# The last pair's chunks copied on chip, its stores issued last, and one head sum behind the first output tile

## The chip, the cores and the metric

One core of one Trainium2 chip runs the whole program. The metric is the device time of one execution in microseconds, as the median over runs; runs of the kernel before were 1549.65, 1552.05 and 1554.65 us.

## The reference

The program computes one decoder layer on 1040 tokens (16 meta tokens and 1024 inputs) of width 1024. What matters here, cut down:

```python
xn = rmsnorm(h, g_pre_mix)
p = xn @ w_in                                # RWKV columns | stick-breaking columns
y_a = rwkv7_group(p_rwkv, ...)               # 8 heads x 64: state scan, group norm, bonus, gate
y_b = stick_breaking_group(q, k, v, gain)    # 8 heads x 64: stick-breaking attention, RMSNorm per head
h = h + rmsnorm(concat(y_a, y_b) @ w_out, g_post_mix)
m = square(relu(rmsnorm(h, g_pre_ffn) @ w_ffn_up)) @ w_ffn_down
h = h + rmsnorm(m, g_post_ffn)               # returned without the meta tokens
```

`rwkv7_group` multiplies its normed result by a gate and adds a bonus, both of which are known before the scan. The stick-breaking output `o` is divided by the root of its mean square per head.

## The kernel before

The program has three large stages, each a block: all five engines leave a block together, after the last of them is done.

**`stage_in_proj`** computes the projection in 26 tiles and, beside it, prepares the RWKV heads in four pairs of heads (`PAIRS`; 128 partitions hold two heads of 64). For each pair it makes `fields`, 17 chunks of 64 tokens with five fields each (B, A, R, K, V), and two full rows, `bv` (the bonus) and `gate`. All of these go to DRAM (`chunk_dram`, `bonus_dram`, `gate_dram`). Projected tiles go to `p_dram`, stored by ACT's queue. The last step of `prepare` for a pair, on SP's queue (L352 to L362), waits for all of the pair's work; for the last pair it then calls `start.load_chunk` (L876), which loads chunk 0 of the next stage: of the first three pairs from `chunk_dram`, of the last pair straight from `fields` in SBUF. Then follow the last pair's three stores. Bonus and gate count on `last_small_left`, for which SP waits at the end of its program (L384); the chunk store counts on `left`, which the next stage waits for. POOL ends its program with `start.load_heads` (L888): nine loads of the values, queries and keys of the first attention pair from `p_dram`.

**`stage_mix`** runs the RWKV scan and the attention side by side. The scan takes 17 laps, one chunk each. A lap has a front (products of the chunk's fields `fld[s]` and their exchanged copy `swp[s]`, s = lap mod 2) and a rear (which updates the state and gives `y`). The attention is cut into numbered ticks ("sticks"), and `program` weaves quarters of them between the slots of a lap in one fixed order on every engine. Lap 0 uses the loaded chunk 0. Lap 1 uses `fld1` and `swp1`, which SP loads after it has waited for `left_done` (L1052 to L1054); the same semaphore is waited for by ACT before its first `high_q` (L1181). The first DVE instruction of tick 4 is the clamp at L1318. The first write of ACT into `y_sb` is at L1165 (`m == 0`).

**`stage_tail`** norms and gates `y` and `o`, projects them with `w_out`, adds the residual, and does the FFN. `head_sums` (L2566) are products with a block of ones: `mean(i)` and `var(i)` for `y`, `osum(i)` for `o`, by section i of the tokens. `project_first` (L2604) makes the first token tile from unrounded operands: eight steps of two 128x512 products (L2614), four on `o` and then four on `y`. Between these two halves stand `mean(2)` and `osum(2)`. `osum(2)` waits for ACT's square of `o` (L2008); ACT's logarithm (L2012) waits for `osum(2)`. DVE's `low_of_w` (L2291) of a late weight tile waits until `project_first` has used the tile. DVE's order there is: the last L2291, `scale_o(2)` (L2272, which waits for `ors_done` from ACT), `deviation(2)` (L2250); then ACT squares the deviation (L2018), and `var(2)` on PE waits for that. `project` of tile 1 (L2600) follows `var(2)`.

Of the kernel before, what the change touches and what calls it, by code (L numbers as in the profile page):

```python
# [11 lines left out]
P = 128  # L12
# [3 lines left out]
SEQ = 1024  # L16
# [4 lines left out]
CH = 64  # L21
# [172 lines left out]
def stage_in_proj(nc, start, stored, left, x_dram, meta, gain_row, ident, w_in, raw, masks, p_dram, xh, xl, vecs, mu_low, w_low_up, chunk_dram, gate_dram,  # L194
# [7 lines left out]
    with ExitStack() as ctx:  # L202
# [62 lines left out]
        rkv_loaded, vec_loaded, wlow_loaded, last_small_left = m.sem("rkv_loaded"), m.sem("vec_loaded"), m.sem("wlow_loaded"), m.sem("last_small_left")  # L265
# [41 lines left out]
        def _(sp):  # L307
# [29 lines left out]
            def prepare(h, u):  # L337
# [18 lines left out]
                if i == PAIRS - 1:  # L356
                    start.load_chunk(sp, fields)
                small_left = last_small_left if i == PAIRS - 1 else left
                sp.dma_start(bonus_dram[i], bv[:, 0:SEQ]).then_inc(small_left, 16)
                sp.dma_start(gate_dram[i], gate).then_inc(small_left, 16)  # L360
                sp.dma_start(chunk_dram[i].rearrange("c p f -> p c f"),
                             fields[:, :, :, :].rearrange("p c f n -> p c (f n)")).then_inc(left, 16)  # L362
# [21 lines left out]
            sp.wait_ge(last_small_left, 2 * 16)  # L384
# [6 lines left out]
        def _(pool):  # L391
# [41 lines left out]
            M.wait(pool, PAIRS - 1, "b1")  # L433
            start.load_heads(pool)
# [402 lines left out]
class MixStart:  # L837
# [38 lines left out]
    def load_chunk(self, sp, fields):  # L876
# [3 lines left out]
        chunk = self.chunk_dram[there, 0].rearrange("q p f -> p q f")  # L880
        sp.dma_start(self.fld0[:, there, X_B:X_I, :].rearrange("p q f n -> p q (f n)"), chunk[:, :, 0:3 * CH]).then_inc(self.loaded, 16)
        sp.dma_start(self.fld0[:, last, X_B:X_I, :], fields[:, 0, F_B:F_K, :]).then_inc(self.loaded, 16)
        for h in range(2):
            here, other = slice(h * HD, (h + 1) * HD), slice((1 - h) * HD, (2 - h) * HD)
            sp.dma_start(self.swp0[other, there, :, :].rearrange("p q f n -> p q (f n)"), chunk[here, :, CH:]).then_inc(self.loaded, 16)
            sp.dma_start(self.swp0[other, last, :, :], fields[here, 0, F_A:, :]).then_inc(self.loaded, 16)
# [21 lines left out]
def stage_mix(nc, start, stored, left_done, chunk_dram, p_dram, masks, ident, pc, y_sb, o_sb, w_out, w_raw, w_late, gate_dram, bonus_dram):  # L908
# [29 lines left out]
    with ExitStack() as ctx:  # L938
# [21 lines left out]
        v = [m.sb(f"v{s}", [P, BLOCKS, P]) for s in range(2)]  # L960
        tri = m.sb("tri", [P, P])
# [7 lines left out]
        a = [m.sb(f"a{i}", [P, SBW]) for i in range(4)]  # L969
# [81 lines left out]

# [1806 lines left out]
```

## Time and profile before

| | |
|---|---|
| median of three runs | 1552.05 us (1549.65 to 1554.65) |
| the profiled execution's own time | 1554.16 us |
| its span in the profile | 1552.4 us |
| granted TensorE clock, mean over the span | 0.984 |
| PE / DVE / ACT / POOL busy | 95% / 68% / 52% / 19% |
| DMA | 258.06 MB, mean 166 GB/s |

A row of the profile gives an engine (PE is TensorE, DVE VectorE, ACT ScalarE, POOL GpSimd, SP SyncE; a q behind the name is its queue) and a line of the kernel. Times are from the start of the span. The projection stage ends on PE near 348 us, the mixing stage runs from 360 to 779 us, and the tail follows.

### The profile page before, as it was taken

What the parts mean: (1) busy time and instruction counts of PE and PEld (TensorE: products, weight loads), DVE (VectorE), ACT (ScalarE), POOL (GpSimd) and SP (SyncE); (2) the same over time, 40 slices, a digit from 0 to 9 for tenths busy, and PEclk for the clock granted to TensorE, in tenths of its full rate; (3) what the DMA queues carried; (4) which work ended last, traced back from release to release, by engine and by line L of the source; (5) the groups of instructions that cost most, each with busy time, mean ns of one, the idle gap of its engine ahead of it and who ended that gap; (6) DMA issues with size and microseconds to landing.
All of it is one profiled execution on the core that took longest, in us unless ns stands there. A gap on an engine that the chain in (4) does not pass through costs nothing. (4 is left out here: it accounts for less than half of the span.)

```text
span 1552.4 us, 36775 instructions
## 1 busy us (share of the span) xinstructions
PE 1468.7 (95%) x15392; PEld 1243.9 (80%) x15392; DVE 1049.3 (68%) x1522; ACT 805.4 (52%) x1396; POOL 300.2 (19%) x307
## 2 busy tenths in 40 slices
PE   6999999995998999999889996999999999999998
PEld 6999999995777777777658875878888888888886
DVE  6244436445878887789766769998888665544555
ACT  6254445344777877778665543333333343433452
POOL 6233425340001011010100004543333000100000
PEclk9999999997999999999999998999999999999999
DMA  4433562646613224121244567798777585675553
GB/s 183 143 125 126 184 233 75 233 124 196 145 34 85 54 51 106 40 51 42 80 96 122 144 222 239 271 306 280 265 250 247 193 305 190 231 271 192 194 183 136
DMA packets 120220, 258.06 MB, mean 166 GB/s; under 512 B 9200, under 2 KB 50288, under 8 KB 119808
## 3 DMA queue, kind: packets, MB, share of 16 engines
q1 hardware_dynamic: 115536, 239.33, 47.4%
q10 hardware_dynamic: 3744, 13.85, 2.2%
q0 software_dynamic: 784, 2.65, 0.7%
q8 instruction: 116, 1.90, 0.5%
q14 instruction: 40, 0.33, 0.1%
HBM read 167.67 MB, written 86.85 MB: 164 GB/s over the span
## 5 line engine op out<-in xcount | busy, mean ns | idle before, releaser
L2415 DVE TENSOR_TENSOR tail_tl<-tail_down_raw,tail_th 128x1024 fp32r<-128x1024 f32 x84 | 102.0, 1256 | 96.2 <-ACT tail_th L2097 96.2
L2097 ACT ACTIVATE tail_th<-tail_down_raw 128x1024 fp32r<-128x1024 f32 x84 | 84.4, 1052 | 129.1 <-PE tail_bank L2701 114.5
L2701 PE MATMUL tail_bank<-tail_th 128*128 128x512 f32 x336 | 131.0, 390 | 0.0
L2701 PE MATMUL tail_bank<-tail_th,tail_tl 128*128 128x512 f32 x336 | 131.0, 390 | 0.0
L2701 PE MATMUL tail_bank<-tail_tl,tail_th 128*128 128x512 f32 x336 | 130.7, 389 | 0.0
L689 PE MATMUL inproj_acc<-xn_xl,inproj_wh 128*128 128x348 f32 (+1 forms) x384 | 123.4, 321 | 0.0
L689 PE MATMUL inproj_acc<-xn_xh,inproj_wl 128*128 128x348 f32 (+1 forms) x384 | 123.2, 321 | 0.0
L689 PE MATMUL inproj_acc<-xn_xh,inproj_wh 128*128 128x348 f32 (+1 forms) x384 | 123.2, 321 | 0.0
L569 DVE TENSOR_TENSOR inproj_wl<-xn_raw,inproj_wh 128x1024 fp32r<-128x1024 f32 x27 | 34.8, 1287 | 94.5 <-ACT inproj_wh L445 94.5
L2631 PE MATMUL tail_bank<-tail_th,tail_ah 128*128 128x512 f32 x240 | 93.8, 391 | 3.2 <-ACT tail_p L2194 1.2
L2631 PE MATMUL tail_bank<-all_mh,tail_ah 128*128 128x512 f32 x212 | 84.9, 400 | 10.5 <-DVE tail_al L2320 10.5
L2631 PE MATMUL tail_bank<-tail_tl,tail_ah 128*128 128x512 f32 x240 | 93.5, 390 | 0.0
L2631 PE MATMUL tail_bank<-tail_th,tail_al 128*128 128x512 f32 x240 | 93.4, 389 | 0.0
L2631 PE MATMUL tail_bank<-all_mh,tail_al 128*128 128x512 f32 x212 | 84.5, 399 | 0.0
L2631 PE MATMUL tail_bank<-all_ml,tail_ah 128*128 128x512 f32 x212 | 84.5, 399 | 0.0
L1982 POOL TENSOR_TENSOR tail_w_quad<-tail_w_quad 128x512 f32<-128x512 f32 x16 | 24.1, 1507 | 310.6 <-DMA tail_w_quad<-in_w_down 310.6
L2701 PEld LDWEIGHTS tail_bank<-tail_th,tail_tl 128*128 128x128 f32 x336 | 63.1, 188 | 13.5
L2701 PEld LDWEIGHTS tail_bank<-tail_tl,tail_th 128*128 128x128 f32 x336 | 63.1, 188 | 13.3
L2701 PEld LDWEIGHTS tail_bank<-tail_th 128*128 128x128 f32 x336 | 63.1, 188 | 13.2
L689 PEld LDWEIGHTS inproj_acc<-xn_xl,inproj_wh 128*128 128x128 f32 x384 | 72.2, 188 | 0.4
L689 PEld LDWEIGHTS inproj_acc<-xn_xh,inproj_wh 128*128 128x128 f32 x384 | 72.2, 188 | 0.3
L689 PEld LDWEIGHTS inproj_acc<-xn_xh,inproj_wl 128*128 128x128 f32 x384 | 72.3, 188 | 0.0
(388 smaller groups left out, 4411.9 us busy)
## 6 DMA issues: line engine op xcount, KB each, us to landing
tail_down_raw<-u_scratch SPq DMA_DIRECT2D x56, 512.0 KB, 3.5
tail_raw<-in_w_up SPq DMA_DIRECT2D x32, 512.0 KB, 6.6
tail_w_quad<-in_w_down SPq DMA_DIRECT2D x16, 1024.0 KB, 8.9
d_scratch<-tail_w_quad SPq DMA_DIRECT2D x16, 1024.0 KB, 8.4
u_scratch<-tail_u_sums SPq DMA_DIRECT2D x16, 1024.0 KB, 5.9
tail_down_raw<-d_scratch SPq DMA_DIRECT2D x32, 512.0 KB, 4.4
xn_raw<-in_w_in SPq DMA_DIRECT2D x27, 512.0 KB, 5.0
p_scratch<-inproj_out ACTq DMA_DIRECT2D x26, 520.0 KB, 2.7
```

Source lines behind the costliest of these rows:

```text
L569: w_low.done(dve.tensor_tensor(wl[s][:, :, :], raw[s][:, :, :], wh[s][:, :, :].bitcast(F32), ALU.subtract), "all")
L689: last = pe.matmul(acc[g][:, 0:size], w[s][:, kt, :], xx[:, kt, col:col + size], start=(kt == 0 and j == 0), stop=(kt == KD - 1 and j == 2))
L1982: done(pool.tensor_tensor(b(D_1), b(B_12), b(B_11), ALU.subtract), D_1)
L2097: act.activation(op_high[b][:, j, :], down_raw[c % len(down_raw)][:, j, :], ACT.Copy).then_inc(down_high, 1)
L2415: dve.tensor_tensor(op_low[b][:, j, :], down_raw[c % len(down_raw)][:, j, :], op_high[b][:, j, :].bitcast(F32), ALU.subtract).then_inc(dow ...
L2631: last = pe.matmul(out[:, :], w[:, o, kt, :], x[:, kt, :], start=(start and kt == 0 and j == 0), stop=(stop and kt == KH - 1 and j == 2), ...
L2701: last = pe.matmul(downs[pass_of(c) % 2][o][:, :], u[:, own_tile], w[:, f * HALF:(f + 1) * HALF], start=(n == 0 and f == 0 and j == 0), st ...
```

## The change

At the end of `stage_in_proj`, SP no longer stores the last pair's bonus, gate and chunks: it only loads chunk 0 and ends. `load_chunk` takes the chunk number and the tiles. POOL waits for the six loads of chunk 0 before it issues its nine loads of the heads. At the start of `stage_mix`, SP waits for chunk 0 and for all nine loads of the heads, then loads chunk 1 with `load_chunk` (six transfers, the last pair's part from `fields`), and issues the three stores behind it. Bonus and gate are waited for by DVE at tick 4, the chunk store by ACT before its first write into `y_sb`, and by SP before it goes on. The tiles `a` move to a lower place in SBUF. In the tail, `osum(2)` stands behind `project_first`.

```diff
                 if i == PAIRS - 1:
-                    start.load_chunk(sp, fields)
-                small_left = last_small_left if i == PAIRS - 1 else left
-                sp.dma_start(bonus_dram[i], bv[:, 0:SEQ]).then_inc(small_left, 16)
-                sp.dma_start(gate_dram[i], gate).then_inc(small_left, 16)
-                sp.dma_start(chunk_dram[i]..., fields...).then_inc(left, 16)
+                    start.load_chunk(sp, fields, 0, start.fld0, start.swp0, start.loaded)
+                    start.last_fields = fields
+                    start.last_pair = (bonus_dram[i], bv[:, 0:SEQ]), (gate_dram[i], gate), (...)
+                else:
...
             program(sp, tile, before, prepare, True)
-            sp.wait_ge(last_small_left, 2 * 16)
...
             M.wait(pool, PAIRS - 1, "b1")
+            pool.wait_ge(start.loaded, 6 * 16)
             start.load_heads(pool)
...
+        a = [m.sb(f"a{i}", [P, SBW]) for i in range(4)]
         tri = m.sb("tri", [P, P])
...
-        a = [m.sb(f"a{i}", [P, SBW]) for i in range(4)]
...
+            sp.wait_ge(start.loaded, 6 * 16)
+            start.wait_values(sp, 0)
+            for p in range(PARTS):
+                start.wait_part(sp, 0, p)
+            start.load_chunk(sp, start.last_fields, 1, fld[1], swp[1], loaded[1])
+            (bonus_out, bonus_in), (gate_out, gate_in), (chunk_out, chunk_in) = start.last_pair
+            sp.dma_start(bonus_out, bonus_in).then_inc(small_left, 16)
+            sp.dma_start(gate_out, gate_in).then_inc(small_left, 16)
+            sp.dma_start(chunk_out, chunk_in).then_inc(left_done, 16)
             sp.wait_ge(left_done, PAIRS * LEFT + 16)
-            load_own(1, 1)
-            load_exchanged(1, 1)
             load_values(1)
...
                 MG.wait(act, m, "y")
+                if m == 0:
+                    act.wait_ge(left_done, PAIRS * LEFT + 16)
...
-                act.wait_ge(left_done, PAIRS * LEFT + 16)
                 high_q(0, 0)
...
                 for now in range(N + SB_LAG + 1):
+                    if now == 4:
+                        dve.wait_ge(small_left, 2 * 16)
...
                         mean(2)
-                        osum(2)
...
             project_first()
+            osum(2)
             var(2)
```

SP's queue where the projection stage ends and the mixing stage begins, before (`mix_swp_78` belongs to chunk 0, `mix_fld` and `mix_swp` without a number to chunk 1; the branch at L202 is the stage's end, the names behind "waits" are semaphores):

```order
L886 DMA mix_swp_78<-inproj_fields 64x256
L359 DMA bonus_scratch<-inproj_prev 128x1024
L360 DMA gate_scratch<-inproj_rkv 128x1024
L361 DMA chunk_scratch<-inproj_fields 128x17x320
L202 UNCONDITIONAL_BRANCH [waits inproj_loaded0,inproj_wlow_loaded,inproj_loaded1,inproj_vec_loaded,inproj_last_small_left]
L1036 UNCONDITIONAL_BRANCH [waits barrier_Pool_Activation_PE_DVE_SP_release]
L856 DMA mix_fld<-chunk_scratch 128x4x192 [waits all_chunks_left]
L862 DMA mix_swp<-chunk_scratch 64x4x256 x2
L874 DMA mix_vt<-p_scratch 128x1040 [waits mix_z_done]
L862 DMA mix_swp_78<-chunk_scratch 64x4x256 [waits mix_mm_front,all_stored1,all_stored0]
```

The same place in the changed kernel:

```order
L889 DMA mix_swp_78<-inproj_fields 64x256
L202 UNCONDITIONAL_BRANCH [waits inproj_loaded0,inproj_loaded1,inproj_wlow_loaded,inproj_vec_loaded]
L1039 UNCONDITIONAL_BRANCH [waits barrier_Pool_Activation_PE_DVE_SP_release]
L884 DMA mix_fld<-chunk_scratch 128x3x192 [waits all_qk_first0,all_qk_first1,all_v_first,all_chunk_loaded]
L885 DMA mix_fld<-inproj_fields 128x192
L888 DMA mix_swp<-chunk_scratch 64x3x256
L889 DMA mix_swp<-inproj_fields 64x256
...
L1061 DMA bonus_scratch<-inproj_prev 128x1024
L1062 DMA gate_scratch<-inproj_rkv 128x1024
L1063 DMA chunk_scratch<-inproj_fields 128x17x320
L877 DMA mix_vt<-p_scratch 128x1040 [waits mix_z_done,all_chunks_left]
L865 DMA mix_swp_78<-chunk_scratch 64x4x256 [waits mix_mm_front,all_stored1,all_stored0]
```

The three stores of the last pair moved from ahead of the stage's end to behind the loads of chunk 1, those loads wait for the nine loads of the heads instead of the chunk store, and the stage's end waits for no store of SP's. (Two rows that repeat are not shown.)

DVE's queue in the mixing stage at the end of lap 0 and the start of lap 1, in the changed kernel (before, the rows and their order are the same, without `all_small_left`):

```order
L1308 TENSOR_TENSOR mix_ks<-mix_k_80,mix_ks 64x2x640 [waits mix_qk_high]
L1275 COPY_PREDICATED mix_zi<-early_masks,mix_bank 128x256 [waits mix_mm_front]
L1331 TENSOR_SCALAR mix_w<-mix_z 128x128 [waits mix_z_copied,all_small_left]
L1331 TENSOR_SCALAR mix_w<-mix_z 128x128 [waits mix_z_copied]
L1337 TENSOR_TENSOR mix_wn<-mix_z,mix_w 128x128 [waits mix_ln_done]
L1254 TENSOR_TENSOR mix_nb<-mix_bank,early_masks 128x4x128 [waits mix_mm_rear,mix_mm_front]
```

Nothing moved here, but the first clamp of tick 4 now waits for the stores of bonus and gate too, and the first product mask of lap 1 (`mix_nb`) stands three rows behind it.

PE's queue in the tail, in `project_first` and behind it, before:

```order
L2614 MATMUL tail_bank<-early_w_late,mixed_o 128x512 x7
L2566 MATMUL tail_bank<-mixed_y,all_ones_bd 128x256 [waits tail_rs_ln,tail_gated]
L2566 MATMUL tail_bank<-mixed_y,all_ones_bd 128x256 x3
L2566 MATMUL tail_bank<-tail_ors,all_ones_bd 128x256 [waits tail_o_squared]
L2566 MATMUL tail_bank<-tail_ors,all_ones_bd 128x256 x3
L2614 MATMUL tail_bank<-early_w_late,mixed_y 128x512 x2
L2614 MATMUL tail_bank<-early_w_raw,mixed_y 128x512 x6
L2566 MATMUL tail_bank<-tail_rsd,all_ones_bd 128x256 [waits tail_dev_squared]
L2566 MATMUL tail_bank<-tail_rsd,all_ones_bd 128x256 x3
L2600 MATMUL tail_bank<-mixed_wh,tail_yh 128x512 [waits tail_ors_ln,tail_wout_low,tail_vec_done,tail_y_low]
```

The same place in the changed kernel:

```order
L2626 MATMUL tail_bank<-early_w_late,mixed_o 128x512 x7
L2579 MATMUL tail_bank<-mixed_y,all_ones_bd 128x256 [waits tail_rs_ln,tail_gated]
L2579 MATMUL tail_bank<-mixed_y,all_ones_bd 128x256 x3
L2626 MATMUL tail_bank<-early_w_late,mixed_y 128x512 x2
L2626 MATMUL tail_bank<-early_w_raw,mixed_y 128x512 x6
L2579 MATMUL tail_bank<-tail_ors,all_ones_bd 128x256 [waits tail_o_squared]
L2579 MATMUL tail_bank<-tail_ors,all_ones_bd 128x256 x3
L2579 MATMUL tail_bank<-tail_rsd,all_ones_bd 128x256 [waits tail_dev_squared]
L2579 MATMUL tail_bank<-tail_rsd,all_ones_bd 128x256 x3
L2613 MATMUL tail_bank<-mixed_wh,tail_yh 128x512 [waits tail_ors_ln,tail_wout_low,tail_vec_done,tail_y_low]
```

The four products of `osum(2)`, which wait for `tail_o_squared`, moved from ahead of the eight products on `mixed_y` to behind them, directly ahead of `var(2)`, which waits for `tail_dev_squared`.

## Rows read from the trace of the kernel before

**Rows 1.** The page, part 1: busy time of PE, its share of the span.

```profile
PE 1468.7 (95%) x15392; PEld 1243.9 (80%) x15392; DVE 1049.3 (68%) x1522; ACT 805.4 (52%) x1396; POOL 300.2 (19%) x307
```

**Rows 2.** Windows: us, length, busy by engine (instructions), granted clock, DMA share, GB/s.

```profile
350.00:355.00 5.00, 0.00 (x0) 0.00 (x0) 0.00 (x0) 0.00 (x0) 0.00 (x0) 0.65 1.06 247
360.00:365.00 5.00, 2.94 (x50) 2.78 (x52) 4.70 (x15) 0.91 (x1) 1.92 (x6) 0.50 1.06 393
```

**Rows 3.** Timeline of SP's queue: start, length, line, transfer.

```profile
338.23 0.62 SPq L881 DMA_DIRECT2D mix_fld<-chunk_scratch  x1
341.59 0.62 SPq L886 DMA_DIRECT2D mix_swp<-inproj_fields  x1
342.89 0.44 SPq L360 DMA_DIRECT2D gate_scratch<-inproj_rkv  x1
```

**Rows 4.** DMA issued in 337 to 348 us: queue, count, KB, us to landing.

```profile
chunk_scratch<-inproj_fields SPq DMA_DIRECT2D x1, 2720.0 KB, 22.6
gate_scratch<-inproj_rkv SPq DMA_DIRECT2D x1, 512.0 KB, 16.2
mix_swp<-inproj_fields SPq DMA_DIRECT2D x2, 64.0 KB, 12.3
```

**Rows 5.** Timeline of POOL around the stage's end.

```profile
338.31 0.76 POOL L874 DMA_DIRECT2D mix_vt<-p_scratch  x1 [1.79 <-issue]
343.17 0.60 POOL L871 DMA_DIRECT2D mix_k<-p_scratch  x1
359.49 0.28 POOL L1088 MEMSET mix_k<- 128x224 f32 x1 [15.72 <-POOLq L202]
```

**Rows 6.** Timeline of PE, first product of the mixing stage; idle before it in brackets.

```profile
360.00 0.48 PE L1371 MATMUL mix_bank<-mix_fld 64*64 64x128 f32 x2 [11.78 <-ACTq L121]
```

**Rows 7.** The same view of DMA, issued in 376 to 377 us.

```profile
mix_swp<-chunk_scratch SPq DMA_DIRECT2D x2, 256.0 KB, 4.4
```

**Rows 8.** The page, part 3: queue, packets, MB, share of 16 engines' span.

```profile
q10 hardware_dynamic: 3744, 13.85, 2.2%
q0 software_dynamic: 784, 2.65, 0.7%
```

**Rows 9.** Timelines of PE and DVE, start of lap 1.

```profile
377.81 0.33 PE L1371 MATMUL mix_bank<-mix_fld 64*64 64x128 f32 x2
376.59 0.22 DVE L1318 TENSOR_SCALAR mix_w<-mix_z 128x128 f32<-128x128 f32 x1
```

**Rows 10.** Timeline of PE in the tail, around `project_first`.

```profile
794.27 1.89 PE L2566 MATMUL tail_bank<-mixed_y,all_ones_bd 128*128 128x256 f32 x8
799.50 3.78 PE L2566 MATMUL tail_bank<-tail_ors,all_ones_bd 128*128 128x256 f32 x8 [3.33 <-ACT tail_ors L2008]
805.99 5.31 PE L2614 MATMUL tail_bank<-early_w_raw,mixed_y 128*128 128x512 f32 x12
811.34 1.99 PE L2566 MATMUL tail_bank<-tail_rsd,all_ones_bd 128*128 128x256 f32 x8
```

**Rows 11.** Timelines of ACT and DVE, same stretch.

```profile
803.31 1.11 ACT L2012 ACTIVATE tail_ors<-tail_bank,tail_eps 128x1024 f32<-128x1024 f32 x1 [3.87 <-PE tail_bank L2566]
804.46 1.06 ACT L2014 ACTIVATE tail_ors<-tail_ors 128x1024 f32<-128x1024 f32 x1
810.23 1.06 ACT L2018 ACTIVATE tail_rsd<-tail_dev 128x1024 f32<-128x1024 f32 x1 [4.72 <-DVE tail_dev L2250]
806.26 1.23 DVE L2291 TENSOR_TENSOR mixed_wl<-early_w_late,mixed_wh 128x1024 fp32r<-128x1024 f32 x1 [3.06 <-PE tail_bank L2614]
807.40 1.66 DVE L2272 SCALAR_TENSOR_TENSOR mixed_o<-mixed_o,tail_vec,tail_ors 128x256 f32<-128x256 f32 x4
```

**Rows 12.** Windows of the same stretch, columns as in Rows 2.

```profile
798.00:799.00 1.00, 0.00 (x0) 0.00 (x0) 1.00 (x3) 1.00 (x2) 0.00 (x0) 0.82 0.00 0
805.00:806.00 1.00, 1.00 (x3) 0.32 (x3) 0.00 (x0) 0.52 (x1) 0.00 (x0) 0.76 0.00 0
```

**Rows 13.** Windows for PE alone: us, length, busy, clock, DMA share, GB/s.

```profile
811.00:831.00 20.00, 19.96 (x91) 1.00 0.51 131
```

More of the change, by code:

```diff
@@ L874, in load_values, with load_chunk @@
         sp.dma_start(self.vt[:, LEAD:], self.p_dram[P_SV + i][:, PAD:TPAD]).then_inc(loaded, 16)
-    def load_chunk(self, sp, fields):
+    def load_chunk(self, sp, fields, n, fld, swp, loaded):
         there, last = slice(0, PAIRS - 1), PAIRS - 1
-        chunk = self.chunk_dram[there, 0].rearrange("q p f -> p q f")
-        sp.dma_start(self.fld0[:, there, X_B:X_I, :].rearrange("p q f n -> p q (f n)"), chunk[:, :, 0:3 * CH]).then_inc(self.loaded, 16)
-        sp.dma_start(self.fld0[:, last, X_B:X_I, :], fields[:, 0, F_B:F_K, :]).then_inc(self.loaded, 16)
+        chunk = self.chunk_dram[there, n].rearrange("q p f -> p q f")
+        sp.dma_start(fld[:, there, X_B:X_I, :].rearrange("p q f n -> p q (f n)"), chunk[:, :, 0:3 * CH]).then_inc(loaded, 16)
+        sp.dma_start(fld[:, last, X_B:X_I, :], fields[:, n, F_B:F_K, :]).then_inc(loaded, 16)
         for h in range(2):
             here, other = slice(h * HD, (h + 1) * HD), slice((1 - h) * HD, (2 - h) * HD)
-            sp.dma_start(self.swp0[other, there, :, :].rearrange("p q f n -> p q (f n)"), chunk[here, :, CH:]).then_inc(self.loaded, 16)
-            sp.dma_start(self.swp0[other, last, :, :], fields[here, 0, F_A:, :]).then_inc(self.loaded, 16)
+            sp.dma_start(swp[other, there, :, :].rearrange("p q f n -> p q (f n)"), chunk[here, :, CH:]).then_inc(loaded, 16)
+            sp.dma_start(swp[other, last, :, :], fields[here, n, F_A:, :]).then_inc(loaded, 16)
     def load_heads(self, eng):
@@ L905, in k_part, with stage_mix @@
     return slice(K_EDGE, KEYS) if p == 0 else slice(0, K_EDGE)
-def stage_mix(nc, start, stored, left_done, chunk_dram, p_dram, masks, ident, pc, y_sb, o_sb, w_out, w_raw, w_late, gate_dram, bonus_dram):
+def stage_mix(nc, start, stored, left_done, small_left, chunk_dram, p_dram, masks, ident, pc, y_sb, o_sb, w_out, w_raw, w_late, gate_dram, bonus_dram):
     ticks = sb_ticks()
@@ L1399, in lap @@
                 if ahead:
[L1400 removed]
+                    pe.wait_ge(loaded[f], (n - f) * (LOADS // 2) + 2 * LOADS)
                     AF.wait(pe, m, "kt")
```

15 lines of the change are left out of this document (9 added, 6 removed).

## The prediction

> **What bounds the kernel now.** I read the page first: PE is busy 95% of the span [rows 1], so a change that moves transfers can only pay where PE stands still. The windows by stretch then show where that is: from 350 to 355 us PE, DVE, ACT and POOL do nothing at all while the DMA engines are full (share 1.06), and the granted clock falls from full to half within that window [rows 2]. A mean of 0.65 over 5 us is 3.5 us at half, so it fell near 351.5 us. The PE timeline gives the hole its length: the first product of the mixing stage comes at 360.00 after 11.78 us of idle, so PE had stopped at 348.22 [rows 6]. Its releaser is printed as an ACT queue entry, which is the stage's barrier. What held the barrier is read from SP's queue and the landings. The store of the gate is issued at 342.89 [rows 3] and lands 16.2 us later [rows 4], at 359.09. POOL, which had issued its last load by 343.77, does its next work at 359.49, and PE at 360.00 [rows 5, 6]. So the last thing that ends the stage is a store nobody there reads, and 0.9 us pass from its landing to PE's first product. Behind the start, PE and DVE carry the mixing stage in one woven order, so I expect a start that is earlier to stay earlier to the end.
>
> The second place is the tail. PE does `mean(2)`, then is idle for 3.33 us until ACT has squared `o`, does `osum(2)` at half clock (3.78 us, where the like `mean(2)` took 1.89), then the products on `y`, and `var(2)` at 811.34 [rows 10]. From 811 us on PE is busy for 19.96 of 20 us at full clock [rows 13].
>
> **The change, part by part.** The profiled execution took 1554.16 us by its own time, the median of the runs is 1552.05. The sum is made against the former; I carry the difference to the median over.
>
> *The stage's end.* Three stores leave it. It then waits for chunk 0's loads, and behind them, because POOL now waits for them, for nine load issues of POOL. The last of the six loads is issued at 341.59 [rows 3]. It took a median of 12.3 us to land for this pair of loads [rows 4], beside nine loads of POOL that were in flight at once; those are now behind it. A larger exchanged load with little beside it took 4.4 us [rows 7]. The new case is nearest to that row, so it lands at 346.0. POOL's nine issues take from 338.31 to 343.77, 5.5 us [rows 5], so POOL is done at 351.5. PE and ACT were done before 350. With the 0.9 us of the barrier, PE starts at 352.4 in place of 360.0: **7.6 us gained**. The bounds: with 12.3 us it would start at 360.3, nothing gained; and PE cannot start sooner than 0.9 us behind its own end at 348.22, which would be 10.9 us.
>
> *The heads' loads.* They start 7.7 us later than before. The page gives the software queue, which carries only these nine, 0.7% of all 16 engines over 1552 us, 10.9 us for 2.65 MB; the ACT queue's store of the last projected tile is one of 26 in 2.2%, 1.3 us [rows 8]. Issued from 346.0, with some 2 us until they are under way, they are all there near 360.4. ACT needs the first half of them at its rounding of the queries, behind lap 0's first products, where they lie well ahead. Cost nothing; the cover is lap 0's front, some 7 us.
>
> *Chunk 1.* Before, it waited for the chunk store, which lands 22.6 us after its issue [rows 4]. Now SP issues its six loads from 360.4, the last 3.4 us later as at chunk 0 (338.23 to 341.59, [rows 3]), and it lands 4.4 us behind, at 368.2. PE wanted chunk 1 at 377.81 [rows 9], now at 370.2. So it is in time by 2.0 us: nothing. That is the thinnest cover of the whole change.
>
> *Bonus and gate.* They are issued at 364.4 and 365.1 and follow chunk 1 in the same queue. At the 393 GB/s that the chunk store alone reaches [rows 2], their 1.05 MB take 2.7 us behind loads that end near 367, so they land near 370.7 with about 1 us of completion. DVE wants its tick-4 clamp at 376.59 [rows 9] less 7.6, that is 369.0. It stalls by 1.7 us. Queued behind it are the other clamp, ACT's exponent and logarithm, which wait for it, and the mask of lap 1. ACT was busy with other work for part of the gap behind that clamp, which gives some of it back: **1.0 us lost**, between 0 (it lands in time) and 8 (below, the slow rival).
>
> *The chunk store.* 2.79 MB at 393 GB/s are 7.1 us, so it lands near 378; ACT's first write to `y_sb` and the loads of chunk 2 come later than that. Nothing. ACT's earlier wait for it had cost nothing either: what ACT waited for then were PE's products. The tiles `a` have another address and the same work.
>
> *The head sum.* Take `osum(2)` away from between, and `y`'s 16 products follow `mean(2)` at once. Twelve took 5.31 us at full clock [rows 10], so 16 take 7.1, from 795.9 to 803.0, and `osum(2)` follows at full clock in 1.9, to 804.8. ACT's logarithm began at 803.31 and its exponent ended at 805.52 [rows 11]; now 804.85 and 807.1. DVE's last late weight tile waited 3.06 us for PE and ended at 807.4 [rows 11]; now it ends at 804.4, but `scale_o(2)` behind it waits for ACT until 807.1. It started at 807.40. So what looks like 3 us freed is 0.3: everything behind, `deviation(2)`, its square at 810.23 and `var(2)` at 811.34, comes **0.3 us earlier**. PE, however, has now nothing to do from 804.8 to 811.0, 6.2 us in one piece. In the trace the clock fell 2.5 us after PE's stop at 796.17 (0.82 in 798 to 799, [rows 12]) and 3.3 us after that at 348.22. So it falls here too. It came back near 805.5 [rows 12], 6.0 us after PE's restart at 799.50; at half speed that is up to 3.0 us of lost work. Before, the half-clock stretch lay in front of `var(2)` and was mostly covered by DVE and ACT. Now it lies on `var(2)` and on the dense products behind it, where PE is the bound [rows 13]. I take 2.7, since the products there are dense from the start; the ends are 0 and 3.0. Net **2.4 us lost**.
>
> The sum: 1554.16 - 7.6 + 1.0 + 2.4 = 1549.96, and against the median 1552.05 - 4.2 = **1547.9 us**.
>
> One rule speaks against the change. The Trainium skill, "DMA: Bandwidth & Descriptors", under "Rules for kernel authors", wants small transfers coalesced, since under 64 KB mostly overhead is paid, and its anatomy section puts that at about 2 us a transfer. Chunk 1 now comes in six pieces down to 64 KB in place of three. By the skill's figure, unhidden, six would cost an estimated 12 us from 360.4 and put PE 2.2 us late, 1550.1 us in all; the row here shows a landing of 4.4 us from issue with others in flight, so these costs overlap.
>
> **The rivals.**
> - *The tail costs nothing.* The clock stays up, or comes back at once. For it: the two falls came 2.5 and 3.3 us after PE's stop, so their timing is not fixed, and how soon it rises is seen once only. Against it: 6.2 us is longer than both. -7.6 + 1.0 - 0.3 = -6.9: 1545.2 us.
> - *Chunk 1 and the small stores come late.* If the loads in six pieces take 9.4 us rather than 4.4 behind the last issue (the contended ones took 12.3), chunk 1 lands at 373.2, 3.0 late, and DVE's stall adds 1 on top. -7.6 + 4.0 + 2.4 = -1.2: 1550.9 us. The 2.0 us of margin speak against it; the software queue's slow drain speaks for it. The rule cited above is this rival's, with about this result.
> - *Slower: the stores share the rings.* If the 2.79 MB chunk store, issued 0.5 us behind the gate, is served beside bonus and gate and not behind them, the gate lands with it: 3.84 MB at 393 GB/s are 9.8 us from 367, with completion 377.8. DVE stands until then, 8.8 late, of which 8.1 pass. -7.6 + 8.1 + 2.4 = +2.9: 1555.0 us. It decides for slower once the gate lands behind 374.9. Against it: in the trace the gate landed after 16.2 and the chunk store after 22.6 us, though issued half a microsecond apart [rows 4], so the queue serves them mostly in order.
> - *It does not do what it says.* If the stage's end is now held by POOL at about the old time (chunk 0 landing after 12 us as before), the start gains nothing, and bonus and gate are later by as much: about 1552.
>
> **How the numbers follow.** 0.3% is 4.7 us, about what a measurement of this kernel tells from no change, so "faster" begins below 1547.4. My forecast has 0.50, with a range of its own of 1546 to 1549.8 from the start (6.5 to 8.6 gained) and the clock; 0.20 of that lies below 1547.4. The free tail has 0.22, late chunk 1 0.17, the slow rival 0.06, no effect 0.05. Faster: 0.20 + 0.22 = 0.42. Same: 0.30 + 0.17 + 0.05 = 0.52. Slower: 0.06. The range goes from 1543.9 (the free tail, a little better) to 1551.9, which takes in late chunk 1 and leaves out the slow rival and the rest.
>
> **What would show it.** In the new profile: PE's first product of the mixing stage at 352 to 353 us, with 4 us of idle before it in place of 11.8. POOL's first load issue near 346. SP's first load of chunk 1 near 360. DVE waiting 1 to 2 us at its first clamp of tick 4. The mixing stage's last PE product 6 to 7 us earlier than 779.5. In the tail an idle of about 6 us before `var(2)`, and the first products of tile 1 at half clock. The prediction is wrong if the barrier is held by something else behind POOL, if PE waits at lap 1 for its chunk, if the stall at tick 4 is over 3 us, if laps absorb the earlier start, or if `var(2)` does not wait.

## The result, and the profile of the changed kernel

The changed kernel takes 1562.27 us in the median of six runs (1558.95 to 1564.31), the kernel before 1552.43 us beside it (1549.65 to 1557.34). The ratio is 1.005 with a 95% interval of 1.0031 to 1.0068: 5 to 11 us slower, where I had forecast 4 us faster. The profiled execution took 1559.4 us (span 1557.7); the one before took 1554.16 us (span 1552.4).

POOL in the changed kernel, timeline (start, length, line, operation; idle before it in brackets):

```profile
345.72 0.76 POOL L877 DMA_DIRECT2D mix_vt<-p_scratch  x1 [9.05 <-DMA mix_swp<-inproj_fields]
350.58 0.60 POOL L874 DMA_DIRECT2D mix_k<-p_scratch  x1
360.99 0.28 POOL L1098 MEMSET mix_k<- 128x224 f32 x1 [9.81 <-POOLq L202]
```

The first two rows are as predicted (346.0 and 351.5). Chunk 0's last load, issued at 341.62, lands 3.4 us later, at 345.0; in the kernel before the same load took 14.0 us (the 12.3 of [rows 4] is the median of two such loads, of 10.6 and 14.0). POOL has issued its nine loads at 351.18. The third is not. POOL goes on 9.8 us later. The DMA view of its last load alone says how far that load had come (queue, count, KB, us from issue to landing):

```profile
mix_k<-p_scratch POOLq DMA_DIRECT2D x1, 264.0 KB, 9.7
```

Issued at 350.58 it lands at 360.28, and POOL follows 0.7 us behind. PE, the same timeline, at the start of the mixing stage and in lap 1:

```profile
361.48 0.48 PE L1384 MATMUL mix_bank<-mix_fld 64*64 64x128 f32 x2 [13.11 <-ACTq L121]
...
385.68 0.37 PE L1384 MATMUL mix_bank<-early_masks,mix_swp 64*64 64x64 f32 x1 [1.04 <-issue]
```

The idle of [rows 6] has grown from 11.8 to 13.1 us. The second row shows a wait that the kernel before does not have: PE stands for 1.04 us in the middle of a group of products, with nothing that it waits for ("issue"). What SP does meanwhile, its queue's timeline and two landings:

```profile
361.11 0.38 SPq L884 DMA_DIRECT2D mix_fld<-chunk_scratch  x1
365.35 0.45 SPq L1062 DMA_DIRECT2D gate_scratch<-inproj_rkv  x1
365.84 0.88 SPq L1063 DMA_DIRECT2D chunk_scratch<-inproj_fields  x1
378.09 0.34 SPq L877 DMA_DIRECT2D mix_vt<-p_scratch  x1
378.54 1.28 SPq L865 DMA_DIRECT2D mix_swp<-chunk_scratch  x2
```

```profile
chunk_scratch<-inproj_fields SPq DMA_DIRECT2D x1, 2720.0 KB, 12.2
gate_scratch<-inproj_rkv SPq DMA_DIRECT2D x1, 512.0 KB, 4.6
```

The chunk store now lands at 378.0, and until then SP waits for it. So the values of pair 1 (L877), which went out at 372.35 before, go out with chunk 2's exchanged fields in one burst at 378.1 to 379.8. Windows of the changed kernel:

```profile
385.00:390.00 5.00, 4.32 (x96) 3.92 (x96) 2.74 (x9) 2.83 (x7) 0.84 (x3) 0.66 0.01 3
812.00:813.00 1.00, 0.00 (x0) 0.00 (x0) 1.00 (x4) 0.00 (x0) 0.00 (x0) 0.66 0.00 0
819.00:820.00 1.00, 1.00 (x5) 0.77 (x5) 0.61 (x1) 0.68 (x1) 0.00 (x0) 0.93 0.00 0
```

Behind the stand of 1.04 us the clock is 0.66 in the mean over 385 to 390, which is 3.4 us at half, or up to 1.7 us of work; in the profile of the kernel before the same window has 1.00. The tail, PE's timeline:

```profile
807.41 1.89 PE L2579 MATMUL tail_bank<-tail_ors,all_ones_bd 128*128 128x256 f32 x8
815.52 3.77 PE L2579 MATMUL tail_bank<-tail_rsd,all_ones_bd 128*128 128x256 f32 x8 [6.22 <-ACT tail_rsd L2031]
```

`osum(2)` at full clock, 6.22 us of idle, `var(2)` at half clock: that is the tail as I had worked it out, against [rows 10]. The clock fell 3.0 us after PE's stop and was back at 819.1, 3.6 us after its restart, where [rows 12] have 6.0. The stretch at half clock is 6.8 us long in both profiles (812.3 to 819.1, and 798.6 to 805.5 before); what differs is how much of it lies ahead of the restart.

### The profile page after: what moved, and what is told of

It is laid out like the page before. It is cut to its first block, busy times and chain, and to the rows that moved or that the text cites. A ratio compares the mean times of both kernels' runs of the same rounds, so it can differ in the third digit from the quotient of the medians.

```text
span 1557.7 us, 36783 instructions
## 1 busy us (share of the span) xinstructions
PE 1468.2 (94%) x15392; PEld 1244.3 (80%) x15392; DVE 1051.0 (67%) x1522; ACT 806.0 (52%) x1396; POOL 297.7 (19%) x307
## 4 chain that ended last, share of the span: by engine, by line
PE 45%; DVE 3%; ACT 1%; issue 1%; DVEq 0%
PE tail_bank L2713 20%; PE tail_bank L2643 18%; PE tail_bank L2613 5%; PE tail_bank L2579 1%; PE tail_bank L2626 1%; DVE tail_tl L2403 1%; PE tail_bank L2636 0%; DVE tail_al L2337 0%; DVE mixed_o L2285 0%; DVE tail_al_f L2355 0%; DVE tail_tl_f L2398 0%; ACT tail_rsd L2031 0%; DVE tail_tl_f L2394 0%; DVE tail_al L2333 0%; DVE tail_dev L2263 0%
## 5 line engine op out<-in xcount | busy, mean ns | idle before, releaser
L2713 PEld LDWEIGHTS tail_bank<-tail_th,tail_tl 128*128 128x128 f32 x336 | 63.1, 188 | 13.4
L2713 PEld LDWEIGHTS tail_bank<-tail_th 128*128 128x128 f32 x336 | 63.1, 188 | 13.1
```

The lines of the kernel that those rows point to most:

```text
L2713: last = pe.matmul(downs[pass_of(c) % 2][o][:, :], u[:, own_tile], w[:, f * HALF:(f + 1) * HALF], start=(n == 0 and f == 0 and j == 0), st ...
```

## The experiments

Each kernel was run beside the kernel before on the same chip, in five rounds. The table has what their traces show: PE's first product of the mixing stage, DVE's mask of the products of laps 1 and 2 (`mix_nb`), `mean(0)`, which opens the tail, and the time from there to the first transposes on PE (`all_ident,tail_t`), which takes in all that the head sum's place changes. Each kernel has one profile. `tail_only`, `chunk2_late` and `values_late` have the program of the kernel before up to 372 us at least, and their starts and that of before differ by 1.1 us; from lap 2 to `mean(0)`, where no experiment changes the program, the fourteen profiles take 379.0 to 383.5 us. So a start is known to about 1 us, and what is left at `mean(0)` only to some 3 us; the ratios rest on 6 to 12 runs of each changed kernel. A ratio is not the quotient of the two medians and can differ from it by 0.15%.

| kernel | start | lap 1 | lap 2 | mean(0) | to transposes | ratio to before |
|---|---|---|---|---|---|---|
| before | 360.00 | 378.98 | 399.07 | 781.19 | 43.2 | 1 |
| changed | 361.48 | 380.57 | 403.23 | 785.73 | 44.6 | 1.0050 (1.0031 to 1.0068) |
| tail_only | 361.13 | 380.05 | 401.43 | 780.87 | 44.2 | 1.0023 (1.0009 to 1.0037) |
| border_only | 362.38 | 381.17 | 402.19 | 784.20 | 41.9 | 1.0023 (1.0008 to 1.0038) |
| heads_at_once | 356.67 | 376.13 | 399.01 | 781.90 | 44.4 | 1.0013 (0.9998 to 1.0028) |
| heads_by_sp | 353.69 | 372.18 | 394.97 | 775.83 | 45.4 | 0.9994 (0.9981 to 1.0007) |
| no_drain | 350.32 | 371.88 | 396.82 | 779.78 | 45.6 | 1.0020 (1.0006 to 1.0034) |
| no_gate_wait | 357.81 | 376.32 | 396.41 | 775.56 | 41.9 | 0.9980 (0.9965 to 0.9996) |
| heads_in_mix | 351.37 | 376.20 | 399.16 | 782.13 | 41.9 | 1.0003 (0.9985 to 1.0020) |
| heads_behind_chunk | 350.88 | 371.31 | 393.82 | 776.45 | 41.9 | 0.9953 (0.9934 to 0.9971) |
| chunk2_late | 360.56 | 379.47 | 400.85 | 780.75 | 41.9 | 1.0004 (0.9990 to 1.0018) |
| values_late | 360.13 | 379.34 | 404.46 | 783.49 | 41.9 | 1.0007 (0.9996 to 1.0018) |
| values_first | 350.97 | 370.47 | 391.94 | 775.48 | 41.8 | 0.9948 (0.9933 to 0.9964) |
| all_by_sp | 350.99 | 377.26 | 397.47 | 779.98 | 41.9 | 0.9973 (0.9961 to 0.9984) |

### The two halves apart

`tail_only` is the kernel before with the head sum moved:

```diff
                         mean(2)
-                        osum(2)
...
             project_first()
+            osum(2)
```

> The kernel before, with only the head sum osum(2) moved behind project_first. Theory (read from the trace of the change, where the tail up to the transposes lost 1.4 us): var(2) starts 0.3 us earlier, behind some 6.2 us of idle PE, at half clock (3.8 us), the clock is back some 3.6 us after PE's restart, and the whole kernel is 1.4 us slower: about 1553.8 against 1552.4. Rival (the tail is the larger part of the loss, since the changed kernel's runs lie 7 to 10 us above and its trace shows only 4.5 us ahead of the tail): 3 us or more slower.

`border_only` is the changed kernel without that move.

> The changed kernel with osum(2) back in its old place: the change of the stage's border alone. Theory: the stage's end is now set by the landing of POOL's heads' loads near 360.3, PE starts near 361.5, PE waits about 1 us for chunk 2's exchanged fields in lap 1 because SP sat in its wait for the chunk store until 378, and the mixing stage ends 4.5 us later than before: about 1557 to 1559. Rival (the head sum carries the loss): within 1 us of the kernel before.

Each costs 0.23%, 3.6 us with an interval of 1.2 to 5.9, and the two make up what the changed kernel lost. `border_only` starts at 362.4 and stands for 0.68 us in lap 1, near what I expected (though for nothing that the profile names), but `mean(0)` comes 3.0 us later than before and not 4.5, and its runs, at 1555.0 us, lie below the 1557 to 1559 that I expected. For the tail my expectation here of 1.4 us was too low, and its fault is in the table: with the head sum in its old place the stretch takes 41.8 to 41.9 us in eight kernels and 43.2 in the profile of before, which I had measured against; in its new place it takes 44.2 to 45.6 in five. The difference is 2.3 to 3.8 us. All five show the same 6.22 us of idle ahead of `var(2)`.

The profile of before is the odd one, and its clock says why: there 6.8 us are at half clock, in the eight others 3.4. In `no_gate_wait`, whose `mean(0)` is at 775.56, the rows of [rows 10] read:

```profile
793.87 2.87 PE L2569 MATMUL tail_bank<-tail_ors,all_ones_bd 128*128 128x256 f32 x8 [3.34 <-ACT tail_ors L2011]
804.46 1.99 PE L2569 MATMUL tail_bank<-tail_rsd,all_ones_bd 128*128 128x256 f32 x8
```

There `var(2)` comes 28.9 us behind `mean(0)`, as in seven of the eight (28.8 in `values_first`); in the profile of before it is 30.15, and in its new place 29.8 in all five. So the move makes `var(2)` 0.9 us later against the usual execution, and 0.4 us earlier only against the one that I had read. The rest is the clock: all five have 6.8 us at half, of which 2.9 to 5.9 us lie behind PE's restart, 1.4 to 2.9 us of work. (0.9 and these make the 2.3 to 3.8.)

### What ends the stage

`heads_at_once` takes POOL's wait for chunk 0 away from the changed kernel; `heads_by_sp` leaves the loads where they are in the program's order and gives them to another queue:

```diff
             M.wait(pool, PAIRS - 1, "b1")
-            pool.wait_ge(start.loaded, 6 * 16)
-            start.load_heads(pool)
...
             program(sp, tile, before, prepare, True)
+            M.wait(sp, PAIRS - 1, "b1")
+            sp.wait_ge(start.loaded, 6 * 16)
+            start.load_heads(sp)
```

> The changed kernel, but POOL issues the nine heads' loads at once (from about 338.3) and not behind chunk 0. Theory (the stage ends when POOL's loads have landed): they land near 355 to 356, as before, since the engines have the same bytes to move, so PE starts near 356.5 and everything behind, chunk 2 included, some 4 to 5 us earlier than in the changed kernel: about 1557. Rival (the stage ends with the last issue of POOL, and something else held it in the changed kernel): PE starts at 349 to 350.

> The changed kernel, but SP's hardware queue issues the nine heads' loads, at the same point (behind chunk 0's landing, ahead of the stage's end). Theory (only POOL's software queue has to be empty at a stage's end): the stage ends at the last issue, 345.7 + 5.8, PE starts at 352 to 353 although the heads land later than that, and the kernel takes about 8 us less than the changed one: 1553 to 1554 (1546 if the whole of it stays). Rival (any queue's loads hold the stage's end until they land, or chunk 0's landing is what is late): PE starts at 356 or later.

The last load in `heads_at_once`, issued at 343.08, and POOL's next work:

```profile
mix_k<-p_scratch POOLq DMA_DIRECT2D x1, 264.0 KB, 12.4
```

```profile
356.19 0.28 POOL L1097 MEMSET mix_k<- 128x224 f32 x1 [12.51 <-POOLq L202]
```

It lands at 355.48, and POOL goes on 0.71 us later, as in the changed kernel. PE starts at 356.67 and the runs take 1556.7 us, both as expected. In `heads_by_sp` the last issue, the last landing and PE's first product are:

```profile
351.49 1.06 SPq L875 DMA_DIRECT2D mix_k<-p_scratch  x1
```

```profile
mix_k<-p_scratch SPq DMA_DIRECT2D x1, 264.0 KB, 9.3
```

```profile
353.69 0.48 PE L1385 MATMUL mix_bank<-mix_fld 64*64 64x128 f32 x2 [3.97 <-ACTq L121]
```

The load lands at 360.8, 7.1 us behind PE's start. So the stage's end waits for the landing of what POOL has in flight, and for the issue alone of what SP has. `no_drain` asks what it is that waits:

```diff
-        block = ctx.enter_context(nc.Block())
+        block = ctx.enter_context(nc.Block(no_gpsimd_drain=True))
```

> The changed kernel with one word more: the block of the projection stage is opened with no_gpsimd_drain=True, so that POOL has no drain instruction at its end. Theory (it is this drain, which the block puts there, that waits until POOL's own loads have landed): POOL's last issue ends near 351.2 as in the changed kernel, the stage ends there, PE's first product comes at 352 to 353 in place of 361.5, as my prediction had it, while the heads still land near 360. Chunk 1 is then issued near 361 as before, bonus and gate land near 370, which DVE wants near 370, chunk 2 and the code block are late as in heads_by_sp (mixing start 353.7, runs 0.9994 of before), so the runs are near 1551 to 1552. Rival (the queue itself or the barrier waits, whatever the block says): PE starts at 361 to 362 and the runs are near 1560.

POOL and PE around the stage's end in `no_drain`:

```profile
350.69 0.64 POOL L874 DMA_DIRECT2D mix_k<-p_scratch  x1
351.27 0.40 POOL L1098 MEMSET mix_k<- 128x224 f32 x1
```

```profile
350.32 0.33 PE L1384 MATMUL mix_bank<-mix_fld 64*64 64x128 f32 x2 [2.03 <-ACTq L121]
```

It is the drain that the block puts at POOL's end: it waits until POOL's own loads have landed. Without it PE starts 2.03 us behind its own last product and does not even wait for POOL's last issue. That is 2.1 us better than the 352.4 of my prediction, and yet the runs are 0.2% slower than before, at 1554.8 us where I expected 1551 to 1552. Its timelines of DVE and then of PE show where it went:

```profile
370.73 0.36 DVE L1331 TENSOR_SCALAR mix_w<-mix_z 128x128 f32<-128x128 f32 x2 [3.13 <-DMA gate_scratch<-inproj_rkv]
```

```profile
391.57 0.27 PE L1384 MATMUL mix_bank<-mix_xx,mix_zi 64*64 64x64 f32 x2 [1.98 <-issue]
401.20 0.21 PE L1384 MATMUL mix_bank<-mix_xx,mix_zi 64*64 64x64 f32 x1 [2.12 <-issue]
```

The gate store lands at 370.7, as predicted, and DVE stands for 3.13 us. PE stands for 4.1 us more in laps 1 and 2. Lap 1 alone takes 4.9 us more than before: 1.98 of the first stand, and two stretches at half clock (375.1 to 378.5 and 392.2 to 395.6) worth 1.7 us of work each. Of 9.7 us gained at the start, 2.25 are left at lap 2 and 1.4 at `mean(0)`; the tail takes more than that.

`no_gate_wait` is the kernel before, in its old order, without the wait that I had found to end the stage:

```diff
             program(sp, tile, before, prepare, True)
-            sp.wait_ge(last_small_left, 2 * 16)
```

with DVE's wait at tick 4, ACT's at `m == 0` and the tiles `a` at their new place, as in the change. (Its lap 1 takes 20.1 us, as before, so neither the tiles' place nor these waits cost anything there.)

> The kernel before with its stores and loads in their old order, but without SP's wait for the gate store at the stage's end: DVE waits for it at tick 4, and ACT's wait for the chunk store is moved to its first write of y (the tiles a have the address they have in the changed kernel). Theory (a stage ends when POOL's loads have landed): the heads land near 355.9 as before, POOL goes on 0.7 us later, PE's first product comes at 356.5 to 357.5 in place of 360, and the runs are 3 us below the kernel before, 1549 to 1550. Rival (the stage's end asks only for the last issue, and the changed kernel's late start has another cause): PE starts at 349 to 350, 1543.

POOL's last load lands at 343.21 + 13.4 = 356.6 and POOL goes on at 357.33, again 0.7 us later. PE starts at 357.8, and the kernel is 0.2% faster than before (0.04 to 0.35). So the gate store did end the stage in the profile of before, at 359.1, but hidden behind it, at 355.9, stood a second landing that I had not priced.

### What is lost in the laps

`chunk2_late` and `values_late` put one wait each into SP's program of the kernel before, to make its loads as late as they are in the changed one:

```diff
+                if n == 2:
+                    MF.wait(sp, 1, "nrb")
                 load_exchanged(n, n % 2)
```

> The kernel before with one more wait: SP issues the exchanged fields of chunk 2 only behind the first product group of lap 1 (about 379 in place of 376.4), where the changed kernel had them for another reason. Theory (what was lost in lap 1 of the changed kernel, 2.6 us, is a stall of about 1 us inside a group of PE products while a block of PE's code comes late through engines that are full with these loads, and the half clock behind it): the code transfer near 381 to 383, PE idle 0.7 to 1.2 us at the products of mix_swp near 384, lap 2 starting 1 to 3 us later than 399.1, the start of lap 1 unchanged; 1 to 2 us in the runs. Rival (lap 1's loss comes from the order of work or the start of the stage): no idle there, lap 2 within 0.5 us of before.

```diff
+            MF.wait(sp, 0, "kt")
             load_values(1)
```

> The kernel before, with SP's load of the values of pair 1 held until the front of lap 0 is done (about 376.4 in place of 372.4), so that it is issued together with chunk 2's exchanged fields, 1 MB in one burst at the start of lap 1, as in the changed kernel. Theory (lap 1 of the changed kernel lost 2.6 us because a block of PE's code, which needs 2.4 to 2.9 us from its transfer to PE's next product, was transferred behind that burst): the transfer on the instruction queue comes near 381 to 382 in place of 378.8, PE stands for 0.7 to 1.5 us inside a group of products near 383, and lap 2 starts 1 to 3 us later than 399.1 with lap 1's start unchanged. Rival (the stall has to do with the changed kernel's own program or its chunk store): no idle, code transfer near 379, lap 2 as in the kernel before.

`chunk2_late` missed: no stand of PE in lap 1, that lap 1.3 us longer than before (as long as in `tail_only`, where it was not touched), nothing at the end and nothing in the runs. Late exchanged fields alone are not the cause. What both have in lap 1 is a stretch at half clock, with no stand ahead of it; the windows of PE alone have in `tail_only` and, behind a stand of 1.49 us, in `heads_behind_chunk`:

```profile
384.00:385.00 1.00, 1.00 (x47) 0.50 0.08 16
```

```profile
381.00:382.00 1.00, 1.00 (x35) 1.00 0.00 0
```

In `tail_only` the clock is at half from 383.4 to 386.8, in `chunk2_late` from 382.9 to 386.3. `border_only`, `heads_in_mix` and `heads_behind_chunk` stand for 0.68, 1.48 and 1.49 us and go on at full clock. `values_late` hit in part. The profile has a queue of its own for instructions, q8, with one transfer every few us here. In the kernel before and in the changed one, the DMA view of 378 to 379 and of 382 to 383:

```profile
q8 instruction: 1, 0.02, 8.5%
```

```profile
q8 instruction: 1, 0.02, 8.7%
```

Finer windows put that transfer at 378.8 in the kernel before and at 382.8 in the changed one. In seven kernels PE stands in lap 1 in the group where it stands in the changed kernel, and goes on 2.4 to 2.9 us behind that transfer (changed: 382.8 and 385.68; `border_only` 383.0 and 385.92; `heads_at_once` 378.6 and 381.42; `heads_by_sp` 375.0 and 377.39; `heads_behind_chunk` 378.0 and 380.71; `heads_in_mix` 383.0 and 385.75; `values_first` 375.8 and 378.66). In the kernel before PE comes there 4 us behind it and has no wait. In `values_late` the transfer moved from 378.8 to 380.8, as expected; PE came there 2.4 us behind it and stood for only 0.3 us, but had 2.80 us to wait at the same kind of place 16 us on, and lap 2 began 5.4 us later than before:

```profile
399.34 0.37 PE L1372 MATMUL mix_bank<-mix_xx,mix_zi 64*64 64x64 f32 x2 [2.80 <-issue]
```

`mean(0)` comes 2.3 us later than before, less than the 4.5 us by which the stretch from lap 2 to there differs between profiles, and the runs show no loss (-0.04 to 0.18%). The kernel before also has such transfers in full stretches without a stand behind them (398.2, at a share of 1.12), and `tail_only` and `chunk2_late` stand for 0.60 and 1.15 us near 404.2. So the burst moves the transfer, as the theory has it, but that it makes the stand is not shown by this run. The Trainium skill, "Runtime: NRT & Kernel Launch", under "Instruction fetch mechanics", has each engine's instructions come in blocks through a DMA queue of their own, mostly hidden. The rows agree that they are hidden in most places; if the stands in the rows are theirs, here they are not.

### Versions that start earlier

All of them have the head sum in its old place, and POOL issues no loads. `heads_in_mix` issues the heads as SP's first work of the mixing stage:

```diff
             sp.wait_ge(start.loaded, 6 * 16)
-            start.wait_values(sp, 0)
-            for p in range(PARTS):
-                start.wait_part(sp, 0, p)
+            start.load_heads(sp)
             start.load_chunk(sp, start.last_fields, 1, fld[1], swp[1], loaded[1])
```

`heads_behind_chunk` issues them on SP directly behind chunk 0, with no wait at the stage's end, and SP waits for neither chunk 0 nor the heads ahead of chunk 1:

```diff
                     start.load_chunk(sp, fields, 0, start.fld0, start.swp0, start.loaded)
+                    M.wait(sp, i, "b1")
+                    start.load_heads(sp)
```

> The changed kernel with the head sum back, and the heads' loads issued by SP's hardware queue as the first thing of the mixing stage, with nothing waited for at the projection's end. Theory: the stage ends with PE's own end, PE starts at 349 to 350, the heads land near 358 and ACT, which wants them near 357, waits 1 us or less; chunk 1, issued from 355.5, bonus and gate then land near 364 to 366, where DVE wants them at 366, and the chunk store lands near 371 to 373, so that chunk 2 (wanted at 376.4 less 10.5) comes 6 us late and takes back 2 to 5 us. Runs 1545 to 1549. Rival (a start this early is lost again in laps 0 and 1, whatever the order): 1551 or more.

> The changed kernel with the head sum back, and the heads' loads issued by SP's hardware queue directly behind chunk 0's, ahead of the stage's end, waiting for nothing. Theory: the nine issues end near 348.3, so the stage ends at 349, PE starts at 349.3 to 350.3, the heads land near 352 to 353, chunk 1 is issued from 349.7, the chunk store lands near 364 to 366, and chunk 2's loads (wanted at 376.4 less 10.5 = 366) are in time: the whole 10 us stay, less 1 for the new places of clock and code. Runs 1542 to 1544. Rival (lost again in the laps): 1548 or more.

In `heads_in_mix` PE starts at 351.4, but in lap 0 it waits for ACT, which waits 2.08 and 3.05 us for the heads:

```profile
362.92 0.90 PE L1543 MATMUL mix_zb<-all_ident,mix_vt 128*128 128x128 f32 x3 [3.28 <-ACT mix_v L1209]
367.89 0.90 PE L1543 MATMUL mix_zb<-all_ident,mix_vt 128*128 128x128 f32 x3 [3.01 <-ACT mix_v L1209]
```

The gain is gone by lap 2, and the runs (1552.8 us) are where the rival had them, not at the 1545 to 1549 of the theory. In `heads_behind_chunk` half of it stays: 1547.07 us against 1552.75, 0.37% faster by these medians and 0.47% (0.29 to 0.66) by the ratio, where I expected 1542 to 1544. Its chunk store needs 17.3 us, so chunk 2 and the values are again one burst at 372.4, with the stand of PE in lap 1. `values_first` parts that burst:

```diff
+            load_values(1)
             sp.wait_ge(left_done, PAIRS * LEFT + 16)
-            load_values(1)
```

`all_by_sp` is `no_gate_wait` with the heads on SP's queue between chunk 0 and the stores.

> The fastest version so far (heads by SP behind chunk 0, no waits at the stage's end, head sum back), but with the values of pair 1 loaded ahead of SP's wait for the chunk store. Theory: chunk 2's loads stay at 372.9, but stand alone, so the block of PE's code comes 1 to 2 us earlier and the stall of 1.5 us at 380.7 goes or shrinks; 1 to 2 us faster, 1545 to 1546. Rival (the stalls of PE's code come from the whole load of the engines, not from this burst): the stall stays or moves, 1547.

> The kernel before with the stores in their old place, no wait for them at the stage's end (as in no_gate_wait), and the heads' loads issued by SP's hardware queue between chunk 0 and the stores; POOL issues none. Theory (with nothing of POOL's in flight the stage ends at SP's last issue): SP's last issue near 350, PE starts at 351 to 352, some 9 us earlier than before, heads landed near 354, the chunk store near 362 to 364, so chunk 1 (six large pieces are three here) and chunk 2 are in time. Runs 1543 to 1545. Rival (chunk 1 or 2 late or code stalls take it back): 1547 to 1550.

The same place of PE's in `heads_behind_chunk`, and then in `values_first`:

```profile
380.71 0.33 PE L1380 MATMUL mix_bank<-early_masks,mix_fld 64*64 64x64 f32 x4 [1.49 <-issue]
```

```profile
378.66 0.33 PE L1380 MATMUL mix_bank<-early_masks,mix_fld 64*64 64x64 f32 x4 [0.28 <-issue]
```

The stand shrinks from 1.49 to 0.28 us with one load moved, and lap 2 begins 1.9 us earlier, of which 1.0 was won in lap 1 and 0.8 ahead of it. A later stand of 2.84 us in lap 2 stays in both, and the runs don't tell the two apart: `values_first` takes 1546.35 us against 1552.19, 0.38% faster by these medians and 0.52% (0.36 to 0.67) by the ratio, the lowest ratio here, within the interval of `heads_behind_chunk`. In `all_by_sp` the chunk store lands only at 368.6, and PE waits at lap 1 for chunk 1:

```profile
375.21 0.47 PE L1375 MATMUL mix_bank<-mix_fld 64*64 64x128 f32 x2 [5.51 <-DMA mix_swp<-chunk_scratch]
```

Its runs, at 1549.4 us, miss the 1543 to 1545 that I expected. That is the place where the changed kernel's copies on chip pay: with them `heads_behind_chunk` starts lap 1 at 371.3 with no such wait, 6 us ahead of `all_by_sp`. The intervals of their ratios overlap, so the runs alone don't show it.

## Why the prediction was wrong

**The step that failed** is "With the 0.9 us of the barrier, PE starts at 352.4", and the line beside it that the heads' loads "cost nothing". I let the stage end with POOL's last issue. It ends with the landing of POOL's last load, at 360.3, because the block drains POOL: +1.5 us in place of -7.6. The heads' own engine time was right (I had them there near 360.4); only who waits for it was not. The evidence lay in front of me and was ambiguous: in [rows 5] POOL stood 15.7 us behind its last issue, and the landings of its loads at 355.9 were hidden by the gate's at 359.1. My last rival named the place (POOL holds the end) with the wrong reason (chunk 0 landing late) and 0.05 of the chance. The bound on the late side should have been "ends when everything in flight has landed", 361 with the barrier; I had not put it into the range. Starts of one program differ by 1.1 us, so how much of the 1.5 us (2.4 in `border_only`) is the change's own is known only roughly.

**The second step** is "so I expect a start that is earlier to stay earlier to the end". `no_drain` had the start and more, and by lap 2 the laps had taken back 7.4 of its 9.7 us. So even with the start that I predicted the sum would have failed.

**Right, and not enough.** POOL's first issue came at 345.72, 0.7 us behind chunk 0's landing (predicted 346.0), POOL's issues ended at 351.2 (351.5), the gate landed 8.8 us behind chunk 1's first issue (9.7 in `no_drain`, at 370.7; I had 10.3 and 370.7), and chunk 1 was in time. The six loads of chunk 1 landed 2.9 to 3.9 us behind their issues, overlapped; so the rule of the Trainium skill that I had set against the change ("DMA: Bandwidth & Descriptors", "Rules for kernel authors") did not decide here. (The 2 us of its anatomy section are given for transfers that POOL issues; these were SP's.) The rival in which the stores share the rings did not come either: the gate landed after 4.6 us, the chunk store after 12.2.

**The gate's stall** was mis-sized: 1.7 us predicted at DVE, none in the changed kernel, since that started late, and 3.13 in `no_drain`, where the start is 2.1 us earlier than I had it.

**The chunk store** was put down as "Nothing", with the reason that the loads of chunk 2 come later than its landing at 378. That doesn't follow from the rows: they went out in 376 to 377 before [rows 7], and with the 7.6 us that I booked they were wanted near 369. SP's wait for the store holds the values of pair 1 and chunk 2, and in lap 1 PE stands, and goes on 2.9 us behind the transfer on the instruction queue that follows their burst. In the changed kernel lap 1 takes 22.7 us from mask to mask in place of 20.1. A stand of 1.04 us and the half clock behind it, up to 1.7 us, make 2.7, which covers the 2.6. Only the stand is new against every profile of the old program: the half clock comes in `tail_only` and `chunk2_late` without a stand and costs that lap 1.3 us there, and three kernels stand without it. With one profile of each kernel it is open what decides when it falls. `values_first` shows the stand shrink when the burst is parted, and `values_late` moved the transfer but made only 0.3 us of stand where it was expected. So that the burst delays a block of PE's instructions is the likeliest reading and not shown; how much of each stand is the transfer's lateness, and how much the block's place in the program, stays open.

**The tail** was right in its mechanism, and its size was partly luck. I predicted 2.4 us; the traces have 2.3 to 3.8, the runs 3.6 (1.4 to 5.7). But against the profile that the sum was made from, the changed kernel lost only 1.4 us: `var(2)` came 0.4 us earlier there, as forecast (0.3), and 3.6 us of half clock behind the restart are 1.8 us of work where I had taken 2.7. The difference to the eight other profiles, in which the old place costs 1.3 us less, made up for it. The half clock lay on `var(2)` and the dense products behind it, as forecast. The free tail, to which I gave 0.22, did not occur in any of five kernels.

## What to carry to other kernels

Before moving a load past a stage's end, ask of each queue whether the end waits for its issue or for its landing, and test that by giving the loads to another queue: here POOL's loads hold the block's end until 0.7 us behind their landing, SP's don't hold it at all. Where an idle has one visible cause, look for the next landing behind it; taking the first away is worth only the distance between the two (here 3.2 us by the landings, 2.2 in PE's start). A move that leaves PE idle for 6 us ahead of dense products cost the clock in five kernels of five. And before a term is read from one profile, a second profile of the same program says how far to trust it: here the first one had 3.4 us more of half clock in the tail than eight others.

## What the runs showed of the hardware

- A drain at a block's end covers POOL's own transfers alone. Four kernels have POOL's next work 0.7 us behind its last landing (360.28 and 360.99, 361.2 and 361.89, 355.48 and 356.19, 356.6 and 357.33). In the last of them SP's gate and chunk stores were still under way (landings at 359.7 and 366.9), and in `heads_by_sp` loads of SP's, the last of which landed at 360.8.
- Without it PE may start while POOL is still issuing (350.32, POOL's last issue ends at 351.33).
- PE can stand inside a group of products with no semaphore to wait for, for up to 3.4 us (`heads_in_mix`, at 404.81), 2.4 to 3.3 us behind a transfer of 0.02 MB on the instruction queue. The transfers in question come while data loads fill the DMA engines (share 1.06 at 382 to 383 in the changed kernel) or directly behind such a burst. Not every such transfer is followed by a stand.
- Idle of 3.3 us ahead of `osum(2)` came with 3.4 us at half clock in eight profiles and with 6.8 in one; idle of 6.2 us ahead of `var(2)` came with 6.8 in all five.
